# Inverse root of the last norm: one GpSimd power in place of ScalarE's root and VectorE's reciprocal

## The chip, the cores and the metric

The kernel runs on one core of a Trainium2 chip. The metric is the device time of one execution in microseconds (us). A core has five engines that run their own instruction streams and meet at semaphores: TensorE (PE in the profile; PEld is its weight load), VectorE (DVE), ScalarE (ACT), GpSimd (POOL) and SyncE (SP), which here only issues transfers.

## The reference, cut to what matters

One layer of a decoder: two attention branches, a mixture of experts, then a last RMS norm over 320 tokens (256 prompt, 64 sample) of 1024 channels. Only the last norm matters here:

```python
def rms_norm(x, g):
    xf = x.astype(jnp.float32)
    y = xf * lax.rsqrt(jnp.mean(xf * xf, axis=-1, keepdims=True) + EPS)
    return (y * g.astype(jnp.float32)).astype(x.dtype)
...
    y_prompt = rms_norm(xp, norm_final_g)
    y_sample = rms_norm(xs, norm_final_g)
```

## The kernel before

Activations are held channel-major: `xT` is 128 partitions x 8 chunks x 320 tokens, chunk k holding channels 128k to 128k + 127. `rstd` is one 128 x 320 tile in which every partition holds the same row, one number for each token. The program is written by hand, engine by engine: each engine's stream is in one fixed order, and a wait stands wherever it needs another engine's result.

The end of the program runs as follows. GpSimd scatters the experts' output rows to memory, pair after pair (L2355). After the last but one pair it waits until all these scatters have landed, writes one throw-away column (L2385) and by that raises `s_ya`; that is its last instruction. SyncE waits for `s_ya` and reads the rows back (L542). VectorE adds the two halves of each row (L2233), TensorE turns them (L1240) and adds the last pair (L1245), and VectorE adds each of the 8 chunks to the residual stream `xT` (`residual`, L1951 to L1954).

The last norm then has six steps. (1) ScalarE squares a chunk as soon as it stands (L1544). (2) TensorE multiplies the squares by a matrix of ones and sums the 8 chunks in `banks[0]`, so each partition gets every token's sum (L1248). (3) VectorE's helper `root(total, n)`, here with n = 3, divides by 1024, adds EPS and writes `rstd` (L1571). (4) ScalarE's helper `rms(n)` takes the square root in place (L1265); ScalarE's stream gets a table load ahead of it. (5) VectorE waits for the root and takes the reciprocal in place (L1573); `link` makes it wait for its own result. (6) VectorE multiplies each chunk by its gain and by `rstd` (L2251), and after every second chunk SyncE sends two chunks out (L546).

`root` and `rms` serve two other norms: `root` and `rms` with n = 1 near the start, `rms` with n = 2 before the experts. The semaphores are `s_ms` (mean square written), `s_rms` (root written) and `s_z` (counts GpSimd's fills; it stands at 8 by the end). `rstd` lies in SBUF, while the sum of squares lies in PSUM.

Of the kernel before, what the change touches and what calls it, by code (L numbers as in the profile page):

```python
# [13 lines left out]
ALU = mybir.AluOpType  # L14
# [3 lines left out]
P = 128  # L18
# [4 lines left out]
N = NP_ + NS  # L23
# [42 lines left out]
C_NEW = C_R + 128  # L66
# [24 lines left out]
def build(nc, vec, x_t, pages, w_ada, w_in, w1, cmp_pages, k_pages, v_pages, win, w_br, w_out,  # L91
          w_ein, w_eout, consts, cond_of, win_state,
          o_y, o_kt, o_small, o_va, o_vs, o_zero, o_win, scratch, h_rows, y_rows):
    with ExitStack() as ctx:
        def sem(name):
            return ctx.enter_context(nc.semaphore(name))
# [29 lines left out]
        def keep(*dims):  # L126

            size = 1
            for d in dims:
                size *= d  # L130
            place[0] += size
            return at(place[0] - size, *dims)


        cst = keep(C_ALL)
# [10 lines left out]
        rstd = keep(N)  # L146
# [183 lines left out]
        x_w = [sem(f"extra_weights_loaded{k}") for k in range(3)]  # L330
        s_ch = sem("vector_chain")
        s_z = sem("gpsimd_zeros_written")
        s_ms, s_rms = sem("mean_square"), sem("root_mean_square")

        block = ctx.enter_context(nc.Block())
# [2 lines left out]
        def page_numbers(engine, first, last):  # L338

            _, numbers = nc.values_load_multi_w_load_instructions(  # L340
                page_row[0:1, first:last], engines=(engine,), min_val=0, max_val=NPHYS - 1,
                skip_runtime_bounds_check_because="a page table holds numbers of pages of the cache")
            return numbers
# [915 lines left out]
        def _(sc):  # L1259
            act = sc.activation  # L1260

            def rms(n):
                sc.wait_ge(s_ms, n)
                part = rstd[64:P, :] if n == 2 else rstd
                act(part, part, ACT.Sqrt).then_inc(s_rms, 1)  # L1265
# [276 lines left out]
            for k in range(KD):  # L1542
                sc.wait_ge(s_x2, KD + k + 1)
                act(sq3[:, k], xT[:, k], ACT.Square).then_inc(s_sq3, 1)  # L1544
            rms(3)


        @block.vector
        def _(ve):
            chain = [0]  # L1550

            def link(ins):

                chain[0] += 1
                ins.then_inc(s_ch, 1)
                ve.wait_ge(s_ch, chain[0])
# [12 lines left out]
            def root(total, n):  # L1569

                ve.tensor_scalar(rstd, total, 1.0 / D, EPS, ALU.mult, ALU.add).then_inc(s_ms, 1)  # L1571
                ve.wait_ge(s_rms, n)
                link(ve.reciprocal(rstd, rstd))  # L1573

            def normed(dst):
                return ve.tensor_tensor(dst, xT, rstd.unsqueeze(1).to_broadcast([P, KD, N]), ALU.mult)
# [70 lines left out]
            ve.wait_ge(s_x, 16)  # L1647
            ve.wait_ge(s_ss, 1)
            root(banks[5][:, 0:N], 1)
            ve.wait_ge(s_pg, 32)  # L1650
            ada_mod(0)
# [575 lines left out]
            def tail():  # L2227

                def row_sums(half, t):

                    tn, part = TOK[t][1], slice(512 * half, 512 * (half + 1))
                    ve.wait_ge(s_yl[3 * half + t], yl_before[3 * half + t] + 32)
                    ve.tensor_tensor(yR[0:tn, t, 0, part], yR[0:tn, t, 0, part], yR[0:tn, t, 1, part], ALU.add).then_inc(s_ysum, 1)  # L2233

                def last_residual(first, last):

                    for c in range(first, last):
                        ve.wait_ge(s_yt, KD + c + 1)
                        residual(c, banks[c], 40, s_x2, KD)

                for t in range(3):
                    row_sums(0, t)
                row_sums(1, 0)
                row_sums(1, 1)
                last_residual(0, 1)
                row_sums(1, 2)
                last_residual(1, KD)
                ve.wait_ge(s_ss3, 1)
                root(banks[0][:, 0:N], 3)
                for k in range(KD):  # L2250
                    ve.scalar_tensor_tensor(xT[:, k, :], xT[:, k, :], gains[:, 2, k:k + 1], rstd, ALU.mult, ALU.mult)\  # L2251
                        .then_inc(s_fin, 1)
# [11 lines left out]
        def _(po):  # L2264
# [118 lines left out]
            for k in range(3):  # L2383
                po.wait_ge(s_ys[k], 16 * ((LAST + 1 - k) // 3))
            po.memset(cst[:, C_SIN:C_SIN + 1], 0.0).then_inc(s_ya, 1)  # L2385


def cond_rows():
# [145 lines left out]
```

## Time and profile before

| what | us |
|---|---|
| median of three runs | 753.07 |
| lowest, highest | 752.62, 753.54 |
| the profiled execution, whole | 755.45 |
| the profiled execution, span from first to last instruction | 753.8 |

The profiled execution lies 2.4 us above the median, and 1.65 us of it lie outside the span. Busy time is time in which an engine executes; the chain of waits follows the end of the program back, at each step to what released it. A group of instructions has one line, engine, operation and shape. "Idle before" is the time that the engine stood still just ahead of an instruction, with what ended it.

### The profile page before, as it was taken

How to read it: one execution, taken by the hardware profiler on the slowest of the kernel's cores; microseconds unless marked ns; L12 is line 12 of the kernel's file. 1: busy time of each engine (PE TensorE's matmuls, PEld its weight loads, DVE VectorE, ACT ScalarE, POOL GpSimd, SP SyncE). 2: the span in 40 equal slices, each digit the busy share in tenths (PEclk: the TensorE clock that was granted, in tenths of full speed). 3: DMA queues.
4: the chain of work that ended last, by engine and by line, in shares of the span. 5: the costliest groups of instructions: out<-in, count | busy, mean ns of one | idle time of the engine just before them, and what ended most of it. 6: DMA issues, size and time to landing. Idle time of an engine off the chain costs nothing.

```text
span 753.8 us, 13479 instructions
## 1 busy us (share of the span) xinstructions
PE 696.9 (92%) x5136; PEld 398.8 (53%) x5136; DVE 278.3 (37%) x886; ACT 172.0 (23%) x410; POOL 84.5 (11%) x127
## 2 busy tenths in 40 slices
PE   5899899999999999799998999999999997888894
PEld 2687577558776665454555776664333332222342
DVE  2553123610102787664530322485411211111256
ACT  0223344112102564322242001331110101010102
POOL 0201000002500343110000000001212121112000
PEclk9999999999999999999999999999999999999998
DMA  8999997717344963899999992438999999999981
GB/s 239 383 411 396 410 366 236 309 68 276 113 157 180 359 256 120 313 363 389 392 378 385 420 407 87 191 104 312 419 418 418 418 419 417 419 419 418 420 254 72
DMA packets 63273, 236.15 MB, mean 313 GB/s; under 512 B 9733, under 2 KB 20878, under 8 KB 48293
## 3 DMA queue, kind: packets, MB, share of 16 engines
q1 hardware_dynamic: 52884, 218.73, 74.9%
q0 software_dynamic: 6432, 14.74, 5.3%
q10 hardware_dynamic: 3888, 1.77, 0.9%
q8 instruction: 43, 0.70, 0.4%
q14 instruction: 26, 0.20, 0.1%
HBM read 230.52 MB, written 19.14 MB: 331 GB/s over the span
## 4 chain that ended last, share of the span: by engine, by line
PE 62%; DMA 16%; SPq 13%; DVE 4%; issue 3%; ACTq 1%; ACT 1%; POOL 0%; POOLq 0%; DVEq 0%
PE bank L628 12%; SPq L485 7%; PE bank L1159 5%; PE bank L1038 5%; PE bank L1022 5%; SPq L504 4%; DMA arena<-in_w_eout 4%; DMA arena<-in_w_in 4%; PE bank L672 3%; PE bank L747 2%; PE bank L1186 2%; PE bank L565 2%; PE bank L970 2%; DMA arena<-h_rows,rows_of_slots_in 2%; PE bank L884 2%
## 5 line engine op out<-in xcount | busy, mean ns | idle before, releaser
L1159 PE MATMUL bank<-arena 128*32 128x512 f32 (+1 forms) x896 | 110.9, 610 | 14.2 <-DMA arena<-in_w_ein 14.0
L628 PE MATMUL bank<-arena 128*128 128x320 f32 x384 | 107.6, 439 | 2.8 <-DMA arena<-in_w_in 2.8
L628 PEld LDWEIGHTS bank<-arena 128*128 128x128 f32 x384 | 72.9, 191 | 34.7 <-DMA arena<-in_w_in 3.1
L1159 PEld LDWEIGHTS bank<-arena 128*32 128x32 f32 (+1 forms) x896 | 31.2, 114 | 82.9 <-issue 77.6
L1186 PE MATMUL bank<-arena 128*32 128x512 f32 (+1 forms) x464 | 58.3, 595 | 4.5 <-DMA arena<-in_w_eout 4.1
L2035 DVE COPY arena<-bank 128x512 f32<-128x512 f32 x14 | 9.7, 692 | 108.0 <-PE bank L1117 108.0
L1488 ACT ACTIVATE arena<-bank 128x256 f32<-128x256 f32 x16 | 6.2, 386 | 149.9 <-PE bank L1159 146.9
L1312 ACT ACTIVATE arena<-bank 32x320 f32<-32x320 f32 x60 | 25.8, 430 | 45.5 <-PE bank L628 45.0
L1038 PE MATMUL bank<-arena 128*128 128x320 f32 x128 | 35.0, 432 | 0.0
L1022 PE MATMUL bank<-arena 128*128 128x320 f32 x128 | 34.8, 432 | 0.0
L1186 PEld LDWEIGHTS bank<-arena 128*32 128x32 f32 (+1 forms) x464 | 15.6, 112 | 36.2 <-issue 29.8
L2355 POOL DMA_INDIRECT y_rows<-arena,rows_of_slots_out x14 | 14.1, 1010 | 151.0 <-DVE arena L2049 135.9
L1038 PEld LDWEIGHTS bank<-arena 128*128 128x128 f32 x128 | 24.1, 189 | 10.2
L1022 PEld LDWEIGHTS bank<-arena 128*128 128x128 f32 x128 | 24.1, 189 | 10.3
L1672 DVE TENSOR_TENSOR arena<-arena 128x320 f32<-128x320 f32 x15 | 7.4, 493 | 54.7 <-ACT arena L1313 54.7
L2049 DVE TENSOR_SCALAR arena<-bank,arena 128x512 f32<-128x512 f32 x15 | 11.3, 751 | 44.1 <-PE bank L1186 44.1
L565 PE MATMUL bank<-arena 128*32 128x128 f32 x768 | 23.7, 273 | 0.2 <-DMA arena<-in_w_ada 0.2
L565 PEld LDWEIGHTS bank<-arena 128*32 128x32 f32 x768 | 20.6, 108 | 4.5 <-issue 4.2
L1951 DVE SCALAR_TENSOR_TENSOR arena<-bank,arena 128x256 f32<-128x256 f32 x24 | 11.6, 483 | 28.0 <-PE bank L1038 24.2
L1357 ACT ACTIVATE arena<-arena 128x128 f32<-128x128 f32 (+1 forms) x48 | 21.1, 444 | 2.6 <-DVE arena L1746 2.6
L672 PE MATMUL bank<-arena 128*128 128x512 f32 (+1 forms) x64 | 21.6, 496 | 0.0
L580 PE MATMUL bank<-arena 128*128 128x256 f32 x64 | 16.5, 411 | 4.5 <-DMA arena<-in_cmp_pages 4.5
(413 smaller groups left out, 1011.5 us busy)
## 6 DMA issues: line engine op xcount, KB each, us to landing
arena<-in_w_ein SPq DMA_DIRECT2D x52, 1024.0 KB, 25.2
arena<-in_w_eout SPq DMA_DIRECT2D x26, 1024.0 KB, 26.9
arena<-in_w_ada SPq DMA_DIRECT2D x12, 2048.0 KB, 14.3
arena<-in_w_in SPq DMA_DIRECT2D x10, 2048.0 KB, 10.4
arena<-in_k_pages SPq DMA_DIRECT2D x64, 320.0 KB, 6.0
arena<-in_v_pages SPq DMA_DIRECT2D x64, 320.0 KB, 9.2
arena<-in_w_ein SPq DMA_DIRECT2D x3, 4096.0 KB, 21.8
arena<-in_w_eout SPq DMA_DIRECT2D x3, 2048.0 KB, 13.1
```

Of the source, the lines that this page charges most:

```text
L485: sp.dma_start(wi2[p % 3][:, u, 4 * part:4 * part + 4].rearrange("p k n -> p (k n)"), w_ein[bass.ds(of[u], 1), :, 2048 * part:2048 * part ...
L504: sp.dma_start(wo2[p % 3][:, u].rearrange("p k n -> p (k n)"), w_eout[bass.ds(of[u], 1), :, :].rearrange("o p n -> (o p) n")).then_inc(s_w ...
L565: m = mm(banks[6 + n % 2][32 * j:32 * (j + 1), 0:P].rearrange("p (c d) -> p c d", d=32), condS[:, k, :], columns[:, j], start=(k == 0), st ...
L580: m = mm(banks[2 * v][:, 0:256].rearrange("p (g j m) -> p g j m", g=2, m=4), w1s[v][:, t, :], odd, start=(t == 0), stop=(t == 7))
L628: m = mm(banks[c % 4][:, 0:N], ring[q][:, k, P * (c % 4):P * (c % 4 + 1)], hT[:, k, :], start=(k == 0), stop=(k == KD - 1))
L672: m = mm(bank[0:tn, 0:width], hT[:, k, t0:t0 + tn], ring[q][:, k, 0:width], start=(k == 0), stop=(k == KD - 1))
L1022: m = mm(banks[2 * (c % 2) + a][:, 0:N], wbr_sb[:, 4 * a + k, P * c:P * (c + 1)], src[:, k, :], start=(k == 0), stop=(k == 3))
L1038: m = mm(banks[4 + c % 2][:, 0:N], wo_sb[:, k, P * c:P * (c + 1)], mT[:, k, :], start=(k == 0), stop=(k == KD - 1))
L1159: m = mm(banks[2 + p % 2][r:r + n, :], xeT[p % 2][:, k, r:r + n], wi2[p % 3][:, e, k, :], start=(k == 0), stop=(k == KD - 1))
L1186: m = mm(banks[6 + half][r:r + n, :], actT[:, p % 2, j, r:r + n], wo2[p % 3][:, e, j, 512 * half:512 * (half + 1)], start=(j == 0), stop=( ...
L1312: act(qr[32 * r:32 * (r + 1), c % 3, :], banks[c % 4][32 * (r ^ 1):32 * (r ^ 1) + 32, 0:N], ACT.Copy)
L1357: m = act(seg, seg, ACT.Exp, bias=st[:, 4 + j:5 + j], scale=SCALE, accum_out=st[:, 8 + j:9 + j])
```

## The change

For the last norm alone, ScalarE's root and VectorE's reciprocal go. GpSimd, after its last write, fills one column with -0.5, waits for that, waits for VectorE's mean square, and raises `rstd` in place to the power -0.5 (a tensor-tensor operation whose second operand is that column, broadcast along the row). It then raises a new semaphore, for which VectorE waits before its 8 multiplications. The other two norms stay as they are.

```diff
+        s_last = sem("last_root")
...
             for k in range(KD):
                 sc.wait_ge(s_x2, KD + k + 1)
                 act(sq3[:, k], xT[:, k], ACT.Square).then_inc(s_sq3, 1)
-            rms(3)
...
                 ve.tensor_scalar(rstd, total, 1.0 / D, EPS, ALU.mult, ALU.add).then_inc(s_ms, 1)
-                ve.wait_ge(s_rms, n)
-                link(ve.reciprocal(rstd, rstd))
+                if n == 3:
+                    ve.wait_ge(s_last, 1)
+                else:
+                    ve.wait_ge(s_rms, n)
+                    link(ve.reciprocal(rstd, rstd))
...
             po.memset(cst[:, C_SIN:C_SIN + 1], 0.0).then_inc(s_ya, 1)
+            power = cst[:, C_NEW:C_NEW + 1]
+            po.memset(power, -0.5).then_inc(s_z, 1)
+            po.wait_ge(s_z, 9)
+            po.wait_ge(s_ms, 3)
+            po.tensor_tensor(rstd, rstd, power.to_broadcast([P, N]), ALU.pow).then_inc(s_last, 1)
```

## Rows read from the trace of the kernel before

**Rows 1.** The page: busy time by engine, then the chain that ended last, by engine.

```profile
PE 696.9 (92%) x5136; PEld 398.8 (53%) x5136; DVE 278.3 (37%) x886; ACT 172.0 (23%) x410; POOL 84.5 (11%) x127
...
PE 62%; DMA 16%; SPq 13%; DVE 4%; issue 3%; ACTq 1%; ACT 1%; POOL 0%; POOLq 0%; DVEq 0%
```

**Rows 2.** Chain of waits, 744 to 754 us: start, length, what held the end.

```profile
743.82 0.28 PE bank L1248
744.11 0.02 issue
744.13 0.50 DVE arena L1571
744.63 0.02 issue
744.66 0.48 ACT arena L1265
745.14 0.02 issue
745.16 2.17 DVE arena L1573
747.33 0.02 issue
747.35 0.07 DVE arena L2251
```

**Rows 3.** Timeline of the end: start, length, engine, line, operation, idle before.

```profile
743.25 1.28 ACT L1265 ACT_TABLE_LOAD   x1
...
744.13 0.49 DVE L1571 TENSOR_SCALAR arena<-bank 128x320 f32<-128x320 f32 x1 [1.40 <-PE bank L1248]
744.66 0.47 ACT L1265 ACTIVATE arena<-arena 128x320 f32<-128x320 f32 x1
745.16 2.15 DVE L1573 RECIPROCAL arena<-arena 128x320 f32<-128x320 f32 x1 [0.54 <-ACT arena L1265]
747.35 3.79 DVE L2251 SCALAR_TENSOR_TENSOR arena<-arena 128x320 f32<-128x320 f32 x8
748.39 3.11 SPq L546 DMA_DIRECT2D out_y<-arena  x4
```

**Rows 4.** Busy time of each engine in four stretches of the end.

```profile
core 0: us, PE busy (x) PEld busy (x) DVE busy (x) ACT busy (x) POOL busy (x), PEclk, DMA share, GB/s
...
744.13:747.35 3.22, 0.00 (x0) 0.00 (x0) 2.65 (x3) 0.87 (x2) 0.00 (x0) 0.96 0.02 5
747.35:751.20 3.85, 0.00 (x0) 0.00 (x0) 3.79 (x8) 0.00 (x0) 0.00 (x0) 0.50 0.48 184
```

**Rows 5.** Timeline of POOL: its last instruction.

```profile
717.86 0.10 POOL L2385 MEMSET arena<- 128x1 f32 x1 [6.84 <-DMA y_rows<-arena,rows_of_slots_out]
```

**Rows 6.** Timeline around 253 us: VectorE releases POOL.

```profile
253.41 0.16 DVE L1769 TENSOR_TENSOR arena<-arena 128x4 f32<-128x4 f32 x1
...
253.67 0.63 POOL L2327 TENSOR_SCALAR arena<-arena 128x128 f32<-128x128 f32 x1 [3.02 <-DVE arena L1769]
```

**Rows 7.** Groups of POOL: busy us, mean ns of one, idle before.

```profile
L2328 POOL TENSOR_SCALAR arena<-arena 128x256 f32<-128x256 f32 x12 | 11.2, 932 | 0.0
...
L2327 POOL TENSOR_SCALAR arena<-arena 128x128 f32<-128x128 f32 x12 | 8.5, 712 | 77.8 <-DVE arena L1761 52.1 <-DVE arena L1766 17.0 <-DVE arena L1769 8.7
...
L2336 POOL MEMSET arena<- 128x320 f32 x1 | 0.4, 367 | 79.8 <-PE bank L988 79.8
...
L2385 POOL MEMSET arena<- 128x1 f32 x1 | 0.1, 99 | 6.8 <-DMA y_rows<-arena,rows_of_slots_out 6.8
```

**Rows 8.** Groups of DVE at 128x320: the reciprocal and the plain operation.

```profile
L1573 DVE RECIPROCAL arena<-arena 128x320 f32<-128x320 f32 x2 | 4.3, 2154 | 1.1 <-ACT arena L1265 1.1
...
L1571 DVE TENSOR_SCALAR arena<-bank 128x320 f32<-128x320 f32 x2 | 1.0, 492 | 5.2 <-PE bank L643 3.8 <-PE bank L1248 1.4
```

**Rows 9.** Groups of ACT at 128x320: the square and the root.

```profile
L1544 ACT ACTIVATE arena<-arena 128x320 f32<-128x320 f32 x8 | 3.8, 470 | 8.5 <-DVE arena L1954 8.5
...
L1265 ACT ACTIVATE arena<-arena 128x320 f32<-128x320 f32 x2 | 0.9, 470 | 6.2 <-DVE arena L1571 6.1
```

## The prediction

> **What bounds the kernel now.** I read the page first: TensorE is busy for 92% of the span and GpSimd for 11% [rows 1]. That average says nothing about the place of this change, because TensorE has finished by then. So the next view is the chain of waits over the last ten microseconds [rows 2]. The reader should see that from the end of TensorE's sums at 744.10 us one piece follows another with 0.02 us between them: the mean square on VectorE, the root on ScalarE, the reciprocal on VectorE, the first multiplication. Nothing runs beside this. In the stretch from 744.13 to 747.35 TensorE has no instruction and GpSimd none [rows 4], so each microsecond added or taken here is one of the total. The timeline gives the pieces their exact ends [rows 3]: the mean square ends at 744.13 + 0.49 = 744.62, the root runs from 744.66 to 745.13, the reciprocal from 745.16 to 747.31, and the first multiplication starts at 747.35. **The piece that the change replaces is therefore 747.35 - 744.62 = 2.73 us long**, and 2.15 of it are the reciprocal.
>
> GpSimd's last instruction ends at 717.96 [rows 5]. It then has 744.62 - 717.96 = 26.7 us with nothing to do before the mean square is ready.
>
> **The change part by part.**
>
> Removed, on the path: root, reciprocal and the three gaps around them, 2.73 us.
>
> Removed, off the path: ScalarE's table load. It runs from 743.25 to 744.53 and ends 0.09 us before the mean square does [rows 3]. It is hidden by TensorE's last sums and the mean square, so its going brings nothing. Had it not been hidden, the most that it could cost is its 1.28 us.
>
> Added, off the path: GpSimd's fill of one column with -0.5 and the wait for it. The fill of one column costs 0.10 us [rows 5], and the 26.7 us of rest hide it. Without that cover it would cost 0.10 us plus its wait. It stands behind the signal to SyncE in GpSimd's order, so the reading back of rows isn't delayed. Nothing of the program is queued behind GpSimd's wait for the mean square: the power is its last work. VectorE's new wait has the 8 multiplications queued behind it, and SyncE's four output transfers wait for those. They move as a block with the end of the power; nothing else is late next.
>
> Added, on the path: VectorE wakes GpSimd, GpSimd works for a time T, GpSimd wakes VectorE. The first handover is in the trace: VectorE's operation ends at 253.57 and GpSimd starts at 253.67 [rows 6], 0.10 us. The second isn't; I take ScalarE's handover to VectorE, 745.13 to 745.16, 0.03 us [rows 3]. It may be the 0.10 us of the other direction, which is 0.07 us of uncertainty and no more.
>
> So the difference is 0.10 + T + 0.03 - 2.73 = **T - 2.60 us**. The whole prediction hangs on T, the time of a power over 128 x 320 on GpSimd. No power and no function other than a multiplication or a fill stands on GpSimd in this trace, so I bound it.
>
> *From below.* GpSimd's multiplication takes 712 ns at 128 columns and 932 ns at 256 [rows 7]. That is (932 - 712) / 128 = 1.72 ns a column, and at 320 columns 0.932 + 64 x 0.00172 = 1.04 us. A power is not less work than a multiplication, and it has a second operand. Only a fill, which reads nothing, is quicker at this size (0.37 us), and that I don't take as possible for more than a few in a hundred.
>
> *From above.* The power has to be put together from simpler steps, each of which waits for the one before. If nothing of one column overlaps with the next, each column costs about what GpSimd needs for its smallest instruction, 99 ns for a fill of one column [rows 7]: 320 x 0.099 = 31.7 us.
>
> *Between them.* The nearest row for a function that one pass doesn't give is VectorE's reciprocal: 2154 ns, where its plain operation at the same size takes 492 ns [rows 8], 4.4 times as much. ScalarE's root, by contrast, costs what its square does, 470 ns each [rows 9]; but that engine has tables for it, as the table load in its stream shows, and GpSimd's stream has none. With the ratio 4.4, one such function on GpSimd would be 4.4 x 1.04 = 4.55 us. A general power is a logarithm, a multiplication and an exponential, two such functions: 2 x 4.55 = **9.1 us, which I take**. It lies nearer to the geometric middle of the two ends (5.7 us) than either end does, and it comes from the only row that shows what a composed function costs beside a plain one. Both ends stay in the range.
>
> The sum: 9.1 - 2.60 = +6.5 us. On the profiled execution that is a span of 753.8 + 6.5 = 760.3 and a whole of 755.45 + 6.5 = 762.0 us; this execution lies 2.4 us above the median of the runs for reasons that have nothing to do with this piece, so I put the difference on the median: 753.07 + 6.5 = **759.6 us**.
>
> *A rule against this row.* GpSimd's only arithmetic here, a multiplication by one number per partition, takes 932 ns for 256 columns where VectorE takes 492 ns for 320 [rows 7, 8]: about twice as long or a little more. The Trainium skill, GPSIMD Engine Reference, section "Performance versus the Vector engine", prices all elementwise work on GpSimd that way: about 2.6 cycles an element at 1.2 GHz for two inputs, and about twice VectorE's time. By that page alone T would be an estimated 320 x 2.6 / 1.2 = 0.69 us plus its dispatch, and the kernel some 1.9 us faster at best. The trace agrees for a multiplication; neither it nor the page shows a power. What such a price would do is the second rival below, worked out from the rows.
>
> **The rivals.** A measurement of this kernel can tell about 0.2%, 1.5 us, from no change (three runs lie 0.9 us apart). So with T - 2.60 the kernel is slower by more than that from T = 4.1 us on, and faster by more than that only below T = 1.1 us.
>
> 1. *A quick composed function.* GpSimd overlaps many columns and needs a short recipe: T between 1.1 and 4.1 us. With VectorE's own 2.15 us for its reciprocal the time is 753.07 + 2.15 - 2.60 = 752.6 us, no change. For it: a multiplication leaves GpSimd at 1.72 ns a column, so it does stream. Against it: T would be at most four times a multiplication's, below even VectorE's ratio for a single function. 0.27.
>
> 2. *The other side: a power costs GpSimd one elementwise pass.* T is then 1.04 us and the time 753.07 + 1.04 - 2.60 = 751.5 us, faster by 0.2%. It decides below T = 1.1 us. For it: the instruction is one operation as the program sees it, as ScalarE's root is one, and that costs no more than a square [rows 9]. Against it: GpSimd shows no tables, and a first price of 1.04 us leaves no room for any extra step. This rival can't go far: even with T at the fill's 0.37 us the kernel gains 2.2 us. 0.10.
>
> 3. *No overlap between columns.* T goes towards 31.7 us, and the time to 753.07 + 31.7 - 2.60 = 782.2 us. For it: the steps of a power hang on each other. Against it: the multiplication's 1.72 ns a column show that simple work isn't done column after column. I give everything above T = 18.2 us (twice the forecast) 0.15.
>
> The change does what it says: the root and the reciprocal leave the path, and GpSimd is at rest long before. No rival comes from that.
>
> **How the numbers follow.** The forecast, T between 4.1 and 18.2 us with 9.1 the likeliest, has 0.48: 753.07 + 4.1 - 2.60 = 754.6 to 768.7 us. That and rival 3 are slower, 0.63; rival 1 is the same, 0.27; rival 2 is faster, 0.10. The range reaches down to rival 2's 751.5 us, below which I leave some 0.05, and up into rival 3, to the geometric middle of 18.2 and 31.7 us, T = 24.0 us, which is 774.5 us and cuts that rival in half. It leaves out some 0.13. It is wide because T is unknown over a factor of thirty.
>
> **What would show it.** In the profile after, the chain of waits should end with mean square, a GpSimd tensor-tensor operation at 128 x 320, and the multiplications, without ScalarE or a reciprocal. If the sum is right, the time from the mean square's end to the first multiplication is T + 0.13 us, and everything from the first multiplication on takes what it took: 3.79 us for the eight [rows 4]. GpSimd's fill should stand near 718 us and cost nothing. The table load ahead of the last root should be gone, without the mean square starting earlier after TensorE's last sum. The prediction is wrong if that GpSimd operation takes less than 4.1 us, and wrong in its mechanism if GpSimd starts late after the mean square, or if the multiplications or the output change their pace.

## The result and the profile after

| | before | changed |
|---|---|---|
| median, us | 753.31 (4 runs, 752.62 to 754.20) | 804.63 (4 runs, 801.46 to 806.35) |
| span of the profiled execution, us | 753.8 | 802.5 |

The ratio is 1.0673, 95% interval 1.0645 to 1.0701: slower by 6.7%, some 51 us. The forecast was slower by 6.5 us, and its range ended at 774.5 us. The sign was right, the size was wrong by a factor of eight; for the sign alone any power longer than 2.6 us would have done.

The chain of waits of the changed kernel at the end (start, length, what held the end) answers to [rows 2]:

```profile
743.23 0.82 PE bank L1249 x2
744.05 0.02 issue
744.07 0.50 DVE arena L1571
744.58 0.02 issue
744.60 0.02 POOLq L2392
744.62 0.07 issue
744.68 51.41 POOLq L94
796.10 0.02 issue
796.12 0.08 DVE arena L2254
```

Up to the mean square it is the chain of before. Then one piece of 51.4 us stands where root and reciprocal stood. The profile files it under GpSimd's sequencer and a helper's line; the timeline of the same stretch (start, length, engine, line, operation, idle before) says what it is:

```profile
718.11 0.10 POOL L2388 MEMSET arena<- 128x1 f32 x1 [6.67 <-DMA y_rows<-arena,rows_of_slots_out]
718.14 0.10 POOL L2390 MEMSET arena<- 128x1 f32 x1
...
744.07 0.49 DVE L1571 TENSOR_SCALAR arena<-bank 128x320 f32<-128x320 f32 x1 [1.40 <-PE bank L1249]
744.72 51.37 POOL L2393 TENSOR_TENSOR arena<-arena 128x320 f32<-128x320 f32 x1 [26.47 <-DVE arena L1571]
796.12 3.79 DVE L2254 SCALAR_TENSOR_TENSOR arena<-arena 128x320 f32<-128x320 f32 x8 [51.55 <-POOL arena L2393]
```

The fill of the exponent stands at 718.14 us, beside the old fill, and hides as forecast. GpSimd rests 26.47 us, starts 744.72 - 744.56 = 0.16 us after the mean square's end, works for 51.37 us, and VectorE starts 0.03 us after it. VectorE's own idle time, 51.55 us, confirms the length of the operation from the side of the engine that waits. From the mean square's end to the first multiplication it is 796.12 - 744.56 = 51.56 us where it was 2.73: **48.8 us more, and the spans differ by 48.7**. The stretches of the end (as in [rows 4]) show that nothing else moved:

```profile
core 0: us, PE busy (x) PEld busy (x) DVE busy (x) ACT busy (x) POOL busy (x), PEclk, DMA share, GB/s
...
744.07:796.12 52.05, 0.00 (x0) 0.00 (x0) 0.49 (x2) 0.00 (x0) 51.37 (x1) 0.53 0.00 1
796.12:799.90 3.78, 0.00 (x0) 0.00 (x0) 3.78 (x8) 0.00 (x0) 0.00 (x0) 0.50 0.46 178
```

For 51 us one engine works alone; the eight multiplications behind it take what they took, 3.8 us. In the groups of GpSimd the one power now outweighs all else that it does:

```profile
L2393 POOL TENSOR_TENSOR arena<-arena 128x320 f32<-128x320 f32 x1 | 51.4, 51369 | 26.5 <-DVE arena L1571 26.5
...
L2331 POOL TENSOR_SCALAR arena<-arena 128x256 f32<-128x256 f32 x12 | 11.1, 929 | 0.0
```

### The profile page after: what moved, and what is told of

The parts are those of the page before. It is cut to its first block, busy times and chain, and to the rows that moved or that the text cites. A ratio compares the mean times of both kernels' runs of the same rounds, so it can differ in the third digit from the quotient of the medians.

```text
span 802.5 us, 13479 instructions
## 1 busy us (share of the span) xinstructions
PE 693.6 (86%) x5136; PEld 397.3 (50%) x5136; DVE 276.1 (34%) x885; ACT 170.1 (21%) x408; POOL 135.9 (17%) x129
## 4 chain that ended last, share of the span: by engine, by line
PE 59%; DMA 14%; SPq 12%; POOLq 7%; DVE 3%; issue 2%; ACTq 1%; ACT 0%; POOL 0%; DVEq 0%
PE bank L629 11%; SPq L486 6%; POOLq L94 6%; PE bank L1160 5%; PE bank L1039 4%; PE bank L1023 4%; SPq L505 4%; DMA arena<-in_w_eout 4%; DMA arena<-in_w_in 3%; PE bank L1187 3%; PE bank L673 3%; PE bank L748 2%; PE bank L566 2%; PE bank L971 2%; DMA arena<-in_cmp_pages 2%
## 5 line engine op out<-in xcount | busy, mean ns | idle before, releaser
L1160 PE MATMUL bank<-arena 128*32 128x512 f32 (+1 forms) x896 | 109.1, 602 | 15.0 <-DMA arena<-in_w_ein 14.9
L1187 PE MATMUL bank<-arena 128*32 128x512 f32 (+1 forms) x464 | 58.3, 595 | 5.9 <-DMA arena<-in_w_eout 5.5
L2393 POOL TENSOR_TENSOR arena<-arena 128x320 f32<-128x320 f32 x1 | 51.4, 51369 | 26.5 <-DVE arena L1571 26.5
L2330 POOL TENSOR_SCALAR arena<-arena 128x128 f32<-128x128 f32 x12 | 8.5, 710 | 77.9 <-DVE arena L1764 52.2
```

The source lines that it names most:

```text
L1160: m = mm(banks[2 + p % 2][r:r + n, :], xeT[p % 2][:, k, r:r + n], wi2[p % 3][:, e, k, :], start=(k == 0), stop=(k == KD - 1))
L1187: m = mm(banks[6 + half][r:r + n, :], actT[:, p % 2, j, r:r + n], wo2[p % 3][:, e, j, 512 * half:512 * (half + 1)], start=(j == 0), stop=( ...
L2393: po.tensor_tensor(rstd, rstd, power.to_broadcast([P, N]), ALU.pow).then_inc(s_last, 1)
```

## The experiments

The place of the loss was clear from the profile: T is 51.4 us. What was not clear is what makes T: the arithmetic of a power, a price per column (theory A); something paid once, at the first power (theory B); the two-operand form with a broadcast operand (theory C); the values. Runs 1 to 9 are edits of the changed kernel, and their diffs are against it, cut at `...`; the first five tell these apart. One warning for reading them: executions differ by some us long before the last norm (the mean square ends at 739.2 us in the profile of run 1 and at 744.6 in that of the changed kernel). So each run is read by the length of the piece, and whole times only where several rounds were run.

**1. The same form, another operation.**

```diff
-            po.tensor_tensor(rstd, rstd, power.to_broadcast([P, N]), ALU.pow).then_inc(s_last, 1)
+            po.tensor_tensor(rstd, rstd, power.to_broadcast([P, N]), ALU.mult).then_inc(s_last, 1)
```

> The power becomes a multiplication by the same broadcast column; the rest of the changed kernel stays. The inverse root is thus left out: the last norm's factor is the mean square times -0.5. Theory A, the 51.4 us are the arithmetic of a power: the operation takes about what a multiplication takes at this size, 1.0 to 1.5 us, and the kernel 753.3 + 1.2 - 2.6 = about 752 us. Theory C, the 51.4 us belong to a two-operand operation on GpSimd with a broadcast operand: it stays near 51 us and the kernel near 804 us.

Measured: 748.96 us, one run. The timeline of GpSimd in this kernel:

```profile
739.38 0.72 POOL L2393 TENSOR_TENSOR arena<-arena 128x320 f32<-128x320 f32 x1 [26.29 <-DVE arena L1571]
```

0.72 us: theory C falls. The form costs next to nothing; 51.37 us against 0.72 is the power itself, 71 times a multiplication, with the rest of the program as it was.

**2. Half the columns.**

```diff
-            po.tensor_tensor(rstd, rstd, power.to_broadcast([P, N]), ALU.pow).then_inc(s_last, 1)
+            po.tensor_tensor(rstd[:, 0:160], rstd[:, 0:160], power.to_broadcast([P, 160]), ALU.pow).then_inc(s_last, 1)
```

> The power runs over 160 of the 320 columns (the other half keeps the mean square). Theory A, a price per column of 51.4 / 320 = 0.161 us: the operation takes 25.7 us, the kernel about 804.6 - 25.7 = 779 us. Theory B, a price paid once, at the first power (its code has to come from somewhere): the operation stays near 50 us, the kernel near 804 us.

Measured: 778.13 us. The timeline of GpSimd:

```profile
744.13 25.87 POOL L2393 TENSOR_TENSOR arena<-arena 128x160 f32<-128x160 f32 x1 [26.75 <-DVE arena L1571]
```

The line through both sizes has the slope (51.37 - 25.87) / 160 = 0.159 us a column and starts at 25.87 - 160 x 0.159 = 0.4 us. Theory A holds, B falls.

**3. A small power ahead of the large one.**

```diff
             po.wait_ge(s_z, 9)
+            po.tensor_tensor(cst[:, C_NEW + 8:C_NEW + 16], ones[:, 0:8], power.to_broadcast([P, 8]), ALU.pow)
             po.wait_ge(s_ms, 3)
```

> A power over 8 columns of ones is added near 718 us, where GpSimd is at rest; the full power follows as before. Theory A: the small one takes 8 x 0.161 = 1.3 us plus a start, the full one 51.4 us again, the kernel about 804 us. Theory B: the small one takes some 50 us, the full one a few us, and the kernel ends some 25 us earlier than 804 us, because 26 us of the first use are hidden.

Measured: 802.40 us. The timeline of GpSimd:

```profile
716.21 1.68 POOL L2392 TENSOR_TENSOR arena<-arena 128x8 f32<-128x8 f32 x1
742.87 51.33 POOL L2394 TENSOR_TENSOR arena<-arena 128x320 f32<-128x320 f32 x1 [24.98 <-DVE arena L1571]
```

The first power is the short one, 1.68 us, and lies on the line of run 2 (0.4 + 8 x 0.159 = 1.7). The second, with a power just behind it, still costs 51.33. No part of T is paid once.

**4. One partition.**

```diff
-            po.tensor_tensor(rstd, rstd, power.to_broadcast([P, N]), ALU.pow).then_inc(s_last, 1)
+            po.tensor_tensor(rstd[0:1, :], rstd[0:1, :], power[0:1].to_broadcast([1, N]), ALU.pow).then_inc(s_last, 1)
```

> The power runs over all 320 columns but one partition of 128 (the other partitions keep the mean square). If GpSimd does its partitions side by side, the operation takes 51.4 us as before and the kernel 804 us. If it does the 16 partitions of a core one after the other, it takes 51.4 / 16 = 3.2 us and the kernel about 754 us. Theory B: near 51 us either way.

Measured: 802.09 us. The timeline of GpSimd:

```profile
742.59 51.37 POOL L2393 TENSOR_TENSOR arena<-arena 1x320 f32<-1x320 f32 x1 [26.30 <-DVE arena L1571]
```

51.37 us again, for one value a column instead of 128. The number of partitions doesn't count, the length of the row does (run 2). `rstd` holds the same row 128 times, so the layout has the longest row possible and gains nothing from the 128 partitions.

**5. The values.** Three small powers in GpSimd's rest, 32 columns each:

```diff
             po.wait_ge(s_z, 9)
+            spare = cst[:, C_NEW + 8:C_NEW + 104]
+            po.memset(cst[:, C_NEW + 1:C_NEW + 2], 1.0).then_inc(s_z, 1)
+            po.wait_ge(s_z, 10)
+            po.tensor_tensor(spare[:, 0:32], ones[:, 0:32], power.to_broadcast([P, 32]), ALU.pow)
+            po.tensor_tensor(spare[:, 32:64], cst[:, C_ROW + 1:C_ROW + 33], power.to_broadcast([P, 32]), ALU.pow)
+            po.tensor_tensor(spare[:, 64:96], cst[:, C_ROW + 1:C_ROW + 33], cst[:, C_NEW + 1:C_NEW + 2].to_broadcast([P, 32]), ALU.pow)
```

> Three powers over 32 columns each are added in GpSimd's rest near 718 us: 1 to the -0.5, then 1..32 to the -0.5, then 1..32 to the 1. The rest is the changed kernel. If each column runs the same steps whatever it holds, each takes 0.37 + 32 x 0.159 = 5.5 us (the line through the powers over 320 and 160 columns) and the full power 51.4 us again; the kernel near 804 us. If easy values leave the steps early, the first or the third is clearly shorter than the second.

Measured: 803.72 us. The timeline of GpSimd:

```profile
718.11 5.46 POOL L2395 TENSOR_TENSOR arena<-arena 128x32 f32<-128x32 f32 x1
723.56 5.42 POOL L2396 TENSOR_TENSOR arena<-arena 128x32 f32<-128x32 f32 x1
728.95 5.41 POOL L2397 TENSOR_TENSOR arena<-arena 128x32 f32<-128x32 f32 x1
```

5.4 to 5.5 us each, 1 to the -0.5 as long as any: for these values the price doesn't depend on what is raised to what.

**6. Nothing in the power's place**, to see what the piece was worth at all:

```diff
                 if n == 3:
-                    ve.wait_ge(s_last, 1)
+                    ve.wait_ge(s_ms, 3)
...
-            power = cst[:, C_NEW:C_NEW + 1]
-            po.memset(power, -0.5).then_inc(s_z, 1)
-            po.wait_ge(s_z, 9)
-            po.wait_ge(s_ms, 3)
-            po.tensor_tensor(rstd, rstd, power.to_broadcast([P, N]), ALU.pow).then_inc(s_last, 1)
```

> Nothing stands in the power's place: root, reciprocal and power are left out, and VectorE multiplies by the mean square itself. This is the floor for any replacement. From the mean square's end to the first multiplication about 0.1 us where the kernel before has 2.73: the kernel 753.2 - 2.6 = 750.6 us. If it gains less, the piece was not alone on the path.

Measured: median 751.92 us against 753.17, ratio 0.9972, interval 0.9954 to 0.9991, that is 2.1 us less, between 0.7 and 3.5. The 2.6 us that were expected lie inside. The timeline of VectorE: the multiplications start 0.04 us after the mean square's end.

```profile
745.35 0.49 DVE L1571 TENSOR_SCALAR arena<-bank 128x320 f32<-128x320 f32 x1 [1.40 <-PE bank L1249]
745.88 3.79 DVE L2254 SCALAR_TENSOR_TENSOR arena<-arena 128x320 f32<-128x320 f32 x8
```

So root and reciprocal were alone on the path to the multiplications, as the prediction had it, and a replacement that keeps the mean square could bring these forward by 2.7 us at most. The end of the kernel doesn't follow in full: from the first multiplication to the end of the span this profile takes 753.7 - 745.9 = 7.8 us, where the kernel before takes 753.8 - 747.35 = 6.4 (run 10 comes back to this).

**7 and 8. ScalarE alone.** Two ways to the inverse root without GpSimd and without the reciprocal, both reading the sums from PSUM so that the mean square on VectorE goes too (EPS is filled into the column that held the exponent):

```diff
+            sc.wait_ge(s_z, 9)
+            sc.wait_ge(s_ss3, 1)
+            act(rstd, banks[0][:, 0:N], ACT.Ln, bias=cst[:, C_NEW:C_NEW + 1], scale=1.0 / D).then_inc(s_rms, 1)
+            sc.wait_ge(s_rms, 3)
+            act(rstd, rstd, ACT.Exp, scale=-0.5).then_inc(s_last, 1)
...
-                ve.tensor_scalar(rstd, total, 1.0 / D, EPS, ALU.mult, ALU.add).then_inc(s_ms, 1)
+                if n < 3:
+                    ve.tensor_scalar(rstd, total, 1.0 / D, EPS, ALU.mult, ALU.add).then_inc(s_ms, 1)
...
-            po.tensor_tensor(rstd, rstd, power.to_broadcast([P, N]), ALU.pow).then_inc(s_last, 1)
+            po.memset(cst[:, C_NEW:C_NEW + 1], EPS).then_inc(s_z, 1)
```

> ScalarE alone: a logarithm that reads the sums straight from PSUM (times 1/1024, plus EPS), then the exponential of -0.5 times that; no mean square on VectorE, no reciprocal, no GpSimd power. Each at ScalarE's 0.47 us: from the last sum's end (744.10 us in the profile before) to the first multiplication about 1.1 us instead of 3.25, the kernel 753.2 - 2.2 = 751.0 us. If the second function needs a table load of its own (1.28 us) on the path, 752.3 us.

The second differs from the first in ScalarE's lines alone:

```diff
+            sc.wait_ge(s_z, 9)
+            sc.wait_ge(s_ss3, 1)
+            act(rstd, banks[0][:, 0:N], ACT.Abs_reciprocal_sqrt, bias=cst[:, C_NEW:C_NEW + 1], scale=1.0 / D).then_inc(s_last, 1)
```

> ScalarE alone, one function: the inverse root of the sums straight from PSUM (times 1/1024, plus EPS). One operation of 0.47 us between the last sum and the first multiplication, about 0.6 us instead of 3.25: the kernel 753.2 - 2.65 = 750.5 us. If the function costs ScalarE several passes, 1 us or more later.

Measured: 754.94 us, ratio 1.0019 (0.9997 to 1.0041), for the logarithm and exponential; 752.60 us, ratio 0.9991 (0.9972 to 1.0011), for the one function. Neither can be told from no change. The timeline of the first shows why it gains nothing:

```profile
740.22 1.28 ACT L1548 ACT_TABLE_LOAD   x1 [0.94 <-PE bank L1249]
741.51 0.53 ACT L1548 ACTIVATE arena<-bank,arena 128x320 f32<-128x320 f32 x1
742.06 1.28 ACT L1550 ACT_TABLE_LOAD   x1
743.35 0.47 ACT L1550 ACTIVATE arena<-arena 128x320 f32<-128x320 f32 x1
743.92 3.79 DVE L2260 SCALAR_TENSOR_TENSOR arena<-arena 128x320 f32<-128x320 f32 x8 [5.15 <-ACT arena L1550]
```

Two table loads of 1.28 us stand on the path, one before each function, where I had allowed for one. The first no longer runs beside TensorE's sums as it did before [rows 3]; it now stands behind the wait for them. From the last sum's end (740.14) to the first multiplication it is 3.8 us instead of 3.25, a loss of 0.5 us. The second version has one load behind the last sum and one function of 0.53 us:

```profile
742.81 1.28 ACT L1548 ACT_TABLE_LOAD   x1 [0.94 <-PE bank L1249]
744.11 0.53 ACT L1548 ACTIVATE arena<-bank,arena 128x320 f32<-128x320 f32 x1
744.74 3.79 DVE L2258 SCALAR_TENSOR_TENSOR arena<-arena 128x320 f32<-128x320 f32 x8 [3.37 <-ACT arena L1548]
```

Its last sum ends at 742.73, so the multiplications start 2.0 us later instead of 3.25. That is 1.2 us won there, but from the first multiplication to the end of the span this profile takes 7.6 us instead of 6.4.

**9. The power over three columns.** Runs 2 to 4 say that a power is cheap where the row is short. So the tokens go on the partitions:

```diff
+        T0 = (0, P, N - P)
+        col, diag = rstd[:, 0:3], sq3[:, 0:2].rearrange("p k n -> p (k n)")[:, 0:3 * P].rearrange("p (t n) -> p t n", n=P)
...
-                    m = mm(banks[0][:, 0:N], ones, sq3[:, k, :], start=(k == 0), stop=(k == KD - 1))
+                    for t in range(3):
+                        m = mm(banks[0][:, t:t + 1], sq3[:, k, T0[t]:T0[t] + P], ones[:, 0:1], start=(k + t == 0), stop=(k + t == KD + 1))
                 m.then_inc(s_ss3, 1)
+                te.wait_ge(s_rms, 3)
+                for t in range(3):
+                    m = mm(banks[1][:, T0[t]:T0[t] + P], ones, diag[:, t], start=True, stop=True)
+                m.then_inc(s_ss3, 1)
...
+                ve.tensor_tensor(diag, ident.unsqueeze(1).to_broadcast([P, 3, P]), col.unsqueeze(2).to_broadcast([P, 3, P]),
+                                 ALU.mult).then_inc(s_rms, 1)
+                ve.wait_ge(s_ss3, 2)
...
-            po.tensor_tensor(rstd, rstd, power.to_broadcast([P, N]), ALU.pow).then_inc(s_last, 1)
+            po.tensor_tensor(col, col, power.to_broadcast([P, 3]), ALU.pow).then_inc(s_last, 1)
```

> The power stays on GpSimd, but the tokens are laid on the partitions: TensorE sums into 3 columns (the squares as weights, one column of ones; the third column covers the last 128 tokens), VectorE's mean square and GpSimd's power run over 128 x 3, VectorE multiplies the identity by them, and TensorE spreads the row over all partitions with ones; VectorE multiplies from PSUM. If the power's price is per column and the partitions are free, it takes 0.37 + 3 x 0.159 = 0.85 us instead of 51.4; with 0.16 for the mean square, some 0.55 for the 384 columns of the identity, some 0.6 for TensorE and handovers of 0.1, about 2.5 us from the last sum to the first multiplication instead of 3.25, the last sum itself some 0.4 us later: the kernel 753.2 - 0.4 = 752.8 us, no change that can be measured. If the power has a fixed price that a short row doesn't show, the operation stays above 10 us and the kernel above 762 us.

Measured: 757.54 us, ratio 1.0054 (1.0031 to 1.0077): slower than the kernel before by 4.1 us (2.3 to 5.8), but 47 us below the changed one. The timeline:

```profile
744.36 0.16 DVE L1578 TENSOR_SCALAR arena<-bank 128x3 f32<-128x3 f32 x1 [2.80 <-PE bank L1252]
744.67 0.90 POOL L2403 TENSOR_TENSOR arena<-arena 128x3 f32<-128x3 f32 x1 [27.76 <-DVE arena L1578]
745.60 0.56 DVE L2260 TENSOR_TENSOR arena<-arena 128x384 f32<-128x384 f32 x1 [1.08 <-POOL arena L2403]
746.21 1.36 PEld L1256 LDWEIGHTS bank<-arena 128*128 128x128 f32 x6 [1.98 <-DVE arena L2260]
746.22 1.65 PE L1256 MATMUL bank<-arena 128*128 128x128 f32 x6 [1.90 <-DVE arena L2260]
```

The power takes 0.90 us, as expected (0.85). What was mis-sized is the detour: TensorE's spreading takes 1.65 us, not 0.6, and its sums, three times the matmuls, end 2.3 us after the last square instead of 0.9. By the profile that is 1.4 us later at the mean square and 747.91 - 744.33 = 3.58 us from there to the multiplications instead of 3.25, 1.7 us in all. From the first multiplication to the end of the span this profile takes 755.6 - 747.9 = 7.7 us instead of 6.4; with that it is 3.0 us, which lies inside the interval of the comparison.

**10. The one function, its tables loaded early.** Against run 8:

```diff
+            act(warm, ones[0:1, 0:1], ACT.Abs_reciprocal_sqrt)
+            sc.wait_ge(s_z, 9)
             for k in range(KD):
...
-            sc.wait_ge(s_z, 9)
             sc.wait_ge(s_ss3, 1)
```

> As the one-function version on ScalarE, but a one-element inverse root stands ahead of the squares, where ScalarE is at rest, so that the table load falls there. If the squares run from the same tables, no load is left on the path: last sum, one operation of 0.53 us, first multiplication, 0.65 us in all instead of 3.25, the kernel 2.6 us below the kernel before, about 750.5 us. If the squares need other tables, a load returns after the last square, ends some 0.4 us after the last sum, and the gain is 2.2 us.

Measured: median 752.02 us against 753.57, ratio 0.9983 (0.9960 to 1.0006). The timeline of ScalarE and VectorE:

```profile
731.79 1.28 ACT L1543 ACT_TABLE_LOAD   x1 [0.36 <-issue]
...
743.94 0.53 ACT L1549 ACTIVATE arena<-bank,arena 128x320 f32<-128x320 f32 x1 [0.90 <-PE bank L1249]
...
744.57 3.79 DVE L2259 SCALAR_TENSOR_TENSOR arena<-arena 128x320 f32<-128x320 f32 x8 [2.03 <-ACT arena L1549]
```

The load falls into ScalarE's rest at 731.79 us, the squares need no other tables, and the last sum's end (743.91) is followed by the multiplications 0.66 us later instead of 3.25. That is the 2.6 us that the profile promised, up to the multiplications; the comparison, 1.3 us less with an interval from 3.0 less to 0.5 more, contains them but doesn't exclude no change. Of the runs that compute the norm it has the shortest way from the last sum to the multiplications.

Part of it is given back behind them. From the first multiplication to the end of the span this profile takes 752.7 - 744.6 = 8.1 us instead of 6.4, so from the last sum to the end it is 8.8 us where it was 9.7: 0.9 us less, not 2.6. SyncE's wait for the last output transfer is longer (waits of SyncE: total, times, longest; the kernel before, then this one):

```profile
SPq L94 <- DMA out_y<-arena: 1.8, 1, 1.8
...
SPq L94 <- DMA out_y<-arena: 2.8, 1, 2.8
```

In every profile a packet of instructions starts 3.1 to 3.7 us after TensorE's last matmul (queue q8, 0.02 MB). The queues that carried something from the first packet of the output to the end of the span (packets, MB, share), in the kernel before (749.2 to 753.8 us), then in this one (746.4 to 752.7 us):

```profile
q1 hardware_dynamic: 576, 1.31, 74.0%
...
q1 hardware_dynamic: 576, 1.31, 54.2%
q8 instruction: 1, 0.02, 1.5%
```

In the kernel before, the packet of instructions runs from 747.5 to 748.4 us and the output starts after it; here it runs from 747.6 to 749.1, within the output. All 13 profiles, one execution each, fit this: in runs 1, 6, 8, 9 and 10 the packet overlaps the output and the stretch from the first multiplication to the end is 7.1 to 8.1 us; in the other eight it doesn't and the stretch is 6.4 to 6.5 us. No run moves the one without the other, so this is not shown as the cause. With the stretch counted in, the profiles of runs 6 to 10 give 1.3 us less, 0.5 more, 0.1 less, 3.0 more and 0.9 less than the kernel before, each inside the interval of its comparison.

**11. The changed kernel again.**

> The changed kernel once more, beside the kernel before on this chip. By the piece in the profiles (mean square's end to first multiplication, 51.6 us after, 2.7 us before) the difference is 48.8 us; the first comparison gave 51.3 us with an interval of about 2.1 us either way. If the power is all of it, the difference comes out near 48.8 us. If something else in the program became slower too, it stays near 51 us.

Measured: median 804.27 us against 753.57, ratio 1.0673 (1.0648 to 1.0698): 50.7 us more, between 48.8 and 52.6. The operation is the same to the hundredth:

```profile
742.36 51.37 POOL L2393 TENSOR_TENSOR arena<-arena 128x320 f32<-128x320 f32 x1 [26.46 <-DVE arena L1571]
```

Both comparisons lie about 2 us above the 48.8 us of the piece, and both intervals just reach it. The profiles show no second place: the mean square ends at 742.2 us in this one and at 744.6 in the first, and the stretch from the first multiplication to the span's end is 6.4 us in both and in the kernel before. TensorE's last sum ends between 741.7 and 744.0 us in the five profiles with a power over 320 columns, and between 738.7 and 745.3 us in the six without a power and with the sums as before. So a second cost of 1 to 3 us is neither shown nor excluded.

## Why the prediction was right on the path and wrong on the price of the power

*What bounds the end.* Right for time that is added: the piece grew by 48.8 us, the span by 48.7. Root and reciprocal were alone on the path to the multiplications; with both gone and nothing in their place these started 2.7 us sooner after the mean square (run 6). For time that is taken away, "each microsecond added or taken here is one of the total" did not hold: in the five profiles where the multiplications start within 2.0 us of TensorE's end, not after 3.25 or more, the stretch from there to the end takes 0.7 to 1.7 us longer (run 10).

*Hidden edits.* Right. The fill of the exponent hides at 718 us, and the going table load moves nothing: the mean square starts 0.02 us after TensorE's last sum before and after.

*The handovers.* 0.10 us was taken for VectorE to GpSimd, 0.16 measured; 0.03 for GpSimd to VectorE, 0.03 measured. The difference is thus T - 2.54 instead of T - 2.60, which is nothing.

*The term that failed is T*: "4.4 x 1.04 = 4.55 us" for one composed function and "2 x 4.55 = 9.1 us, which I take". It is 51.37 us, 0.159 us a column (runs 2, 3 and 5). The step carried a ratio over from VectorE, whose reciprocal is 4.4 times its plain operation. GpSimd's power is 71 times its multiplication (run 1). With two such functions the forecast made it 9.1 / 1.04, about 9 times. So the ratio of one engine did not carry over to the other. Of what steps GpSimd makes a power no run shows.

*Both bounds failed too.* The floor, 1.04 us, came from GpSimd's other multiplications, but a multiplication in the change's own form takes 0.72 us (run 1). The ceiling, "each column costs about what GpSimd needs for its smallest instruction, 99 ns", gave 31.7 us; a column of a power costs 1.6 times that. That row was a fill, which computes nothing, and so it bounds a start, not a calculation. With a ceiling that is no ceiling, the range of 751.5 to 774.5 us could not hold 804.6. The forecast's own sign of being wrong looked only downwards, at a power below 4.1 us; the miss went upwards.

*The rivals.* The third, no overlap between columns, came nearest: the price is proportional to the row and indifferent to the partitions (runs 2 and 4). It had 0.15, and its 782.2 us were still 22 us short. Whether the columns don't overlap or each simply has that many steps, these runs don't tell. The second, one elementwise pass, falls with run 1 beside the changed kernel: the same form costs 0.72 us as a multiplication. By the Trainium skill (GPSIMD Engine Reference, "Performance versus the Vector engine") a two-operand pass would cost an estimated 0.69 us plus its dispatch; run 1's 0.72 us agrees for a multiplication. The power doesn't follow it: 51.37 us.

*What a measurement can tell.* I put it at 0.2%, from three runs that lay 0.9 us apart. Later runs of the kernel before lay between 749.5 and 758.3 us, and intervals from three to five rounds are about 0.2% to either side. A gain of 2.6 us, 0.35%, stands at the edge of that, and the 1 us or so that the profiles of runs 6 and 10 leave of it lies below.

## What to carry to other kernels

An operation that an engine can do in one instruction isn't thereby one pass: before a function moves to an engine that shows none in the trace, time that function alone, over a few columns and at two sizes, which takes two rows and gives the price per column and the start. On GpSimd a power costs 0.4 us and 0.16 us for each column of the row, on one partition or on 128. By that line it could pay here only up to (2.54 - 0.4) / 0.159 = 13 columns, and only for values that already lie so: laying them out so cost more than it saved (run 9). For an inverse root over a long row, ScalarE's own function straight from PSUM, with its tables loaded in an earlier rest, leaves 0.66 us between the last sum and the multiplications. Read such a gain at the end of the span too: of the 2.6 us won there, run 10's profile kept 0.9.

## What the runs showed of the hardware that was not expected

- GpSimd's power over 1 partition takes as long as over 128: 51.37 us both times (run 4).
- Its time hardly varies: 51.33 to 51.37 us for 320 columns in five profiles, and 5.41 to 5.46 us for 32 columns whether 1 or 1 to 32 is raised, to -0.5 or to 1.
- Logarithm and exponential got a table load each, 1.28 us, one right behind the other's function (run 7). The Trainium skill (ScalarE: Activation LUTs, "Table sets: the hidden batching unit") names a set that holds both, so that one load would do; the trace shows two, and it decides. Squares, on the other hand, ran from the inverse root's tables without a load (run 10).
- A packet of instructions starts 3.1 to 3.7 us after TensorE's last matmul in every profile; in the five where it falls into the output transfers, these end 0.7 to 1.7 us later (run 10).
